# Spill x unscaled and scale it in parts, run the fourth up unit by quarter products, and project dt with v

## What is computed

```python
# layer 0, input projection: dt is the last 16 columns of w_in
u = h @ p["w_in"]
q1, q2, k1, k2, v, z, xbc, dt = jnp.split(u, cuts, axis=-1)
xbc = jax.nn.silu(centred_dwconv(xbc, p["conv_w"], p["conv_b"]))
dt = jax.nn.softplus(dt + p["dt_bias"].reshape(-1))
...
# both layers, after the mixer
x = layer_norm(ALPHA * x + m[2] * d, p["ln1_g"], p["ln1_b"])
f = jnp.square(jax.nn.relu(modulate(x, m[3], m[4]) @ p["w_up"])) @ p["w_down"]
x = layer_norm(ALPHA * x + m[5] * f, p["ln2_g"], p["ln2_b"])
```

## Time and profile before

| what | value |
|---|---|
| median of three runs | 1444.24 us |
| span of the profiled execution | 1442.8 us |
| TensorE busy | 1397.0 us, 97% of the span |
| TensorE weight loads busy | 1240.1 us, 86% |
| VectorE busy | 1040.2 us, 72% |
| ScalarE busy | 543.1 us, 38% |
| GpSimd busy | 77.3 us, 5% |
| mean granted TensorE clock | 0.997 |
| chain that ended last, by engine | PE 79%, DVE 10%, ACT 5% |

### The profile page before, as it was taken

How to read it: one execution, slowest core, us unless ns; L and a number is a source line. 1 busy time by engine, 2 the same in 40 slices (tenths; PEclk the granted TensorE clock), 3 DMA queues, 4 the chain that set the end, 5 groups by cost and what they waited for, 6 DMA issues and landing times.

```text
span 1442.8 us, 22837 instructions
## 1 busy us (share of the span) xinstructions
PE 1397.0 (97%) x8806; PEld 1240.1 (86%) x8806; DVE 1040.2 (72%) x1651; ACT 543.1 (38%) x982; POOL 77.3 (5%) x146
## 2 busy tenths in 40 slices
PE   4999999999999999999999999999999999999996
PEld 3899988766779998998899879888999889989985
DVE  3694566777568876776776796877887677667778
ACT  4333343367454332332232254434443223223322
POOL 1300000010201000000000111001000000000011
PEclk9999999999999999999999999999999999999998
DMA  9701234696713312321221723551332122123141
GB/s 316 232 30 60 88 118 133 213 310 228 265 45 137 126 59 83 94 87 59 87 88 58 268 88 114 185 185 37 146 103 85 62 88 88 59 87 116 59 160 73
DMA packets 132300, 177.47 MB, mean 123 GB/s; under 512 B 4170, under 2 KB 104258, under 8 KB 131698
## 3 DMA queue, kind: packets, MB, share of 16 engines
q1 hardware_dynamic: 123250, 146.46, 31.4%
q0 software_dynamic: 7376, 26.76, 5.3%
q10 hardware_dynamic: 1584, 3.01, 0.6%
HBM read 166.94 MB, written 9.27 MB: 122 GB/s over the span
## 4 chain that ended last, share of the span: by engine, by line
PE 79%; DVE 10%; ACT 5%; issue 2%; DMA 2%; SPq 1%; POOL 0%; ACTq 0%; DVEq 0%
PE ps L801 40%; PE ps L1325 20%; PE ps L783 5%; PE ps L792 4%; PE ps L832 2%; DVE convT L2024 2%; PE ps L1133 2%; DVE wlo L1926 1%; ACT h_full L1722 1%; SPq L570 1%; DVE p_pad L2691 1%; DMA raw_more<-in_w_mod_l 1%; ACT tmp L1722 1%; ACT whi L1430 1%; PE ps L1144 1%
## 5 line engine op out<-in xcount | busy, mean ns | idle before, releaser
L1430 ACT ACTIVATE whi<-raw 128x512 fp32r<-128x512 f32 (+2 forms) x193 | 178.6, 935 | 357.8 <-PE ps L801 293.6
L801 PE MATMUL ps<-whi,hid_hi 128*128 128x512 f32 x640 | 249.6, 390 | 0.0
L801 PE MATMUL ps<-wlo,hid_hi 128*128 128x512 f32 x640 | 249.2, 389 | 0.0
L801 PE MATMUL ps<-whi,hid_lo 128*128 128x512 f32 x640 | 249.1, 389 | 0.0
L1926 DVE TENSOR_TENSOR wlo<-raw,whi 128x512 fp32r<-128x512 f32 (+2 forms) x193 | 204.9, 1070 | 26.0 <-ACT whi L1430 22.5
L2357 DVE TENSOR_TENSOR acc<-acc,ps 128x512 f32<-128x512 f32 x120 | 80.2, 684 | 122.0 <-PE ps L801 122.0
L801 PE MATMUL ps<-whi,h_hi 128*128 128x256 f32 (+1 forms) x480 | 157.4, 328 | 2.5 <-DVE wlo L1926 1.4
L801 PE MATMUL ps<-whi,h_lo 128*128 128x256 f32 (+1 forms) x480 | 152.9, 319 | 0.0
L801 PE MATMUL ps<-wlo,h_hi 128*128 128x256 f32 (+1 forms) x480 | 152.8, 318 | 0.0
L801 PEld LDWEIGHTS ps<-whi,hid_hi 128*128 128x128 f32 x640 | 120.1, 188 | 25.4 <-DVE wlo L1926 0.8
L801 PEld LDWEIGHTS ps<-whi,hid_lo 128*128 128x128 f32 x640 | 120.1, 188 | 25.1
(11 more groups left out here) (339 smaller groups left out, 2654.6 us busy)
## 6 DMA issues: line engine op xcount, KB each, us to landing
raw<-in_w_up_l SPq DMA_DIRECT2D x32, 1024.0 KB, 5.6
raw<-in_w_down_l SPq DMA_DIRECT2D x32, 1024.0 KB, 4.9
raw<-in_w_mod_l SPq DMA_DIRECT2D x26, 1024.0 KB, 5.8
raw<-in_w_in_l SPq DMA_DIRECT2D x12, 1024.0 KB, 5.2
raw_split<-in_w_mod_l SPq DMA_DIRECT2D x8, 1024.0 KB, 6.7
raw<-in_w_out_l SPq DMA_DIRECT2D x6, 1024.0 KB, 5.9
x_spill<-x_tok POOLq DMA_DIRECT2D x10, 512.0 KB, 2.9
x_tok<-x_spill POOLq DMA_DIRECT2D x10, 512.0 KB, 6.2
```

Of the source, the lines that this page charges most:

```text
L801: mm = pe.matmul(out, a_of(still, k), w_of(part, k), start=(first and k == 0 and part == 0 and still == 0), stop=(last and k == nk - 1 and ...
L1430: act.activation(ring_piece(whi, w, g), piece(w, g), ACT.Copy).then_inc(hi_done, 1)
```

## The change

**x in parts.** `rescale` in the MLP is gone. Pool spills each tile as soon as PE has turned it, unscaled. When all five have landed, ten parts of 128 tokens by 512 columns go one after the other through two buffers that lie in the place of the MLP's gate: load, scale on DVE (two operations on 512 columns), store to the same place, wait for the store, load the part after next. g and b are loaded for 512 columns at a time, the second time when part 4 is scaled. On DVE parts 0 to 3 stand behind groups of downs 0 and 1, parts 4 to 9 behind groups of downs 2 and 3. The gate is spread after the tenth part.

**Unit 3 by quarter products.** SU goes from 4 to 3. The token sums stand behind the first units, the weight sums and halves of unit 3 beside unit 2. The ring's halves are assigned anew, as there are three whole units ahead in place of four.

**dt with v.** dt's 16 columns stand behind the 256 of the first v block in buffers of their own, so the first five groups have 272 columns. ACT copies 16 columns more of each of them. The dt stage and `turn_dt` are gone. The split of block 5 on DVE goes ahead of the convolution of block 7, and the tanh of blocks 6 and 7 on ACT behind groups 2 and 4; the ACT steps of softplus stand at groups 4, 5 and 7 in place of 4, 6 and 8. Counts of semaphores follow.

```diff
--- before.py
+++ after.py
...
         tmp = at("tmp", 192, [P, 2, D])
+        part_g, part_b, part_x0, part_x1 = (at(name, 168 + 2 * n, [P, 512]) for n, name in
+                                            enumerate(("part_g", "part_b", "part_x0", "part_x1")))
+        part_x = (part_x0, part_x1)
...
-        wdt2 = at("wdt_halves", 168.5, [P, KT, 32], F32R)
+        wv = [at(name, kb, [P, KT, BW + 16], F32R) for name, kb in (("v_dt_hi", 48), ("v_dt_lo", 108))]
...
-        SU, NS_UP, CONV_UP = 4, 12, 8
+        SU, NS_UP, CONV_UP = 3, 13, 6
...
-        PAR = [w % 2 for w in W_UP]
...
+        def half(w):
+
+            return (w + sum(w > u + SU for u in W_UP)) % 2
+
+        PAR = [half(w + SU) for w in W_UP]
...
-            r = [4 * (w % 2) + n for n in range(4)]
+            r = [4 * half(w) + n for n in range(4)]
...
+            if w == W_V:
+                return (wv[0] if buf is whi else wv[1])[:, :, 0:BW]
             ap = at_ring(buf, ring(w)[g])
...
             def spill_x(layer):
 
                 for t in range(NT):
-                    pool.wait_ge(ln_x, 2 * NT * layer + t + 1)
+                    pool.wait_ge(ln_tr, 2 * NT * layer + t + 1)
                     pool.dma_start(A["x_spill"][t * P:(t + 1) * P, :], x[:, t, :]).then_inc(x_re, 16)
 
+            def part_in_memory(n):
+
+                cols = slice(n // NT * 512, n // NT * 512 + 512)
+                return A["x_spill"][n % NT * P:(n % NT + 1) * P, cols]
...
+            def load_part(layer, n):
+
+                if n % NT == 0:
+                    pool.wait_ge(ln_x, 3 * NT * layer + n)
+                    for which, dst in (("g", part_g), ("b", part_b)):
+                        pool.dma_start(dst[:], A[f"ln1_{which}_l{layer}"][n // NT * 512:n // NT * 512 + 512]
+                                       .partition_broadcast(P)).then_inc(gb_ld, 16)
+                pool.dma_start(part_x[n % 2][:], part_in_memory(n)).then_inc(part_ld[n % 2], 16)
+
+            def scale_parts(layer):
+
+                spilled = 16 * NT * (4 * layer + 2)
+                pool.wait_ge(x_re, spilled)
+                load_part(layer, 0)
+                load_part(layer, 1)
+                for n in range(2 * NT):
+                    pool.wait_ge(ln_x, 3 * NT * layer + n + 1)
+                    pool.dma_start(part_in_memory(n), part_x[n % 2][:]).then_inc(x_re, 16)
+                    pool.wait_ge(x_re, spilled + 16 * (n + 1))
+                    if n + 2 < 2 * NT:
+                        load_part(layer, n + 2)
+
             def fetch_x_again(layer):
 
                 pool.wait_ge(up_mm, UPS * layer + CONV_UP + NS_UP * NPROD)
-                pool.wait_ge(x_re, 16 * NT * (2 * layer + 2))
                 for t in range(NT):
                     pool.dma_start(x[:, t, :], A["x_spill"][t * P:(t + 1) * P, :]).then_inc(x_re, 16)
-                load_gb(2 * layer + 1)
...
             def mlp(layer):
 
                 spill_x(layer)
+                scale_parts(layer)
+                spread_gate(2 * layer + 1)
                 fetch_x_again(layer)
 
-            load_gb(0)
             norm_share(0)
-            spread_gate(1)
             mlp(0)
...
-            pe.wait_ge(dt_wl, 1)
-            pe.wait_ge(mod_row, M_MIX)
-            pe.wait_ge(mod_out, M_MIX)
-            for k in range(KT):
-                for part, n in ((1, 16), (0, 32)) if k else ((0, 32), (1, 16)):
-                    for hf in range(2):
-                        mm = pe.matmul(ps[0:n, (6 + hf) * 512:(6 + hf) * 512 + HALF], wdt2[:, k, 0:n],
-                                       HP[part][:, k, hf * HALF:(hf + 1) * HALF],
-                                       start=(k == 0 and part == 0), stop=(k == KT - 1 and part == 0))
-            mm.then_inc(dt_row, 1)
...
-            def turn_dt():
-
-                pe.wait_ge(dt_cp, 1)
-                rows = dtT[:].rearrange("p a n -> p (a n)")
-                for t in range(NT):
-                    mm = pe.transpose(bank(6, 32 * t, 32 * t + 32), rows[0:32, t * P:(t + 1) * P], ident[0:32, 0:32])
-                mm.then_inc(dt_mm, 1)
...
+                if ib == 0:
+                    pe.wait_ge(dt_wl, 1)
+                    tokens_still(bank(4 + g % 2, 0, BW + 16), h_tile(HP, t), lambda part, k: wv[part][:, k, :], KT) \
+                        .then_inc(ib_mm, 1)
+                    return
...
-                if g == 1:
-                    turn_dt()
...
-                    if u == SU and item == 0:
-                        pe.wait_ge(relu_ok[layer], 8 * (layer + 1))
+                    if u == SU and item in (0, 2):
+                        pe.wait_ge(relu_ok[layer], 2 * SU * (layer + 1) - (1 if item == 0 else 0))
...
-                    if f >= 1:
+                    if 1 <= f < KT - 1:
                         conv_tanh(f - 1)
...
+                if ib == 0:
+                    act.activation(dx[:, 16 * t:16 * t + 16], bank(4 + g % 2, BW, BW + 16), ACT.Copy)
                 act.activation(v[:, 2 + t, ib * BW:(ib + 1) * BW], bank(4 + g % 2, 0, BW), ACT.Copy).then_inc(v_ev, 1)
...
-                if g == 1:
-                    conv_tanh(KT - 1)
+                if g in (2, 4):
+                    conv_tanh(KT - 3 + g // 2)
                 if g == 4:
                     act.wait_ge(dt_v, 2)
...
-                if g == 6:
+                if g == 5:
...
-                if g == 8:
+                if g == 7:
...
+                if g == 8:
...
-                        split_hi(w + 1)
+                        split_hi(w + 1, None, (0, 1, 2))
                         relu_square(layer, 2 * n)
-                        if n == 3:
-                            for m, (k0, hf) in enumerate(((4, 1), (0, 0), (0, 1), (4, 0))):
-                                high_t(layer, m, k0, hf)
+                        for m, (k0, hf) in enumerate(((4, 1), (0, 0), (0, 1), (4, 0))):
+                            high_t(layer, m, k0, hf)
                         relu_square(layer, 2 * n + 1)
+                        split_hi(w + 1, None, (3, 4, 5))
                         continue
...
+                    if f == 5:
+                        dve.wait_ge(dt_w, 2)
+                        dve.tensor_tensor(wv[1][:, :, BW:BW + 16], wdt[:], wv[0][:, :, BW:BW + 16].bitcast(F32),
+                                          ALU.subtract).then_inc(dt_wl, 1)
+                    if f == KT - 1:
+                        split_lo(5)
                     conv(f)
                     if f >= 1:
                         conv_silu(f - 1)
-            split_lo(5)
             conv_silu(KT - 1)
...
+            dve.wait_ge(v_ev, NT)
+            dve.tensor_tensor(dx3, dx3, db[:, 0, :].unsqueeze(1).to_broadcast([P, NT, 16]), ALU.add).then_inc(dt_v, 1)
             dve.wait_ge(dt_v, 1)
-            mark(dve.tensor_tensor(dx3, dx3, db[:, 0, :].unsqueeze(1).to_broadcast([P, NT, 16]), ALU.add))
...
+            def scale_part(layer, n):
+
+                dve.wait_ge(gb_ld, 32 * (3 * layer + n // NT + 1))
+                dve.wait_ge(part_ld[n % 2], 16 * (NT * layer + n // 2 + 1))
+                mark(dve.tensor_tensor(part_x[n % 2][:], part_x[n % 2][:], part_g[:], ALU.mult))
+                settle()
+                dve.tensor_tensor(part_x[n % 2][:], part_x[n % 2][:], part_b[:], ALU.add).then_inc(ln_x, 1)
...
                 dve.wait_ge(t_hi, 4 * layer + n + 1)
-                if n == 0:
-                    dve.wait_ge(ln_x, NT * (2 * layer + 1))
                 if n == 2:
...
-                    if n >= 4:
-                        rescale(2 * layer, n - 4)
+                token_sums(layer)
...
-                        split_lo(w + 1)
+                        weight_sums(w + 1)
+                        split_lo(w + 1, None, (0, 1, 2))
+                        dve.wait_ge(gate_out, 16 * (2 * layer + 2))
                         square_low(layer, 2 * n)
-                        if n == 2:
-                            rescale(2 * layer, 4)
-                        else:
-                            low_t(layer, 0, 4, 1, tlo[:, 0])
-                            low_t(layer, 1, 0, 0, tlo[:, 1])
+                        low_t(layer, 0, 4, 1, tlo[:, 0])
+                        low_t(layer, 1, 0, 0, tlo[:, 1])
                         square_low(layer, 2 * n + 1)
-                        if n == 2:
-                            token_sums(layer)
-                        else:
-                            low_t(layer, 2, 0, 1, hhi[:, 0:4, HALF:TOK])
-                            low_t(layer, 3, 4, 0, hlo[:, 0:4, HALF:TOK])
-                            dve.wait_ge(t_lo, 4 * (layer + 1))
+                        low_t(layer, 2, 0, 1, hhi[:, 0:4, HALF:TOK])
+                        split_lo(w + 1, None, (3, 4, 5))
+                        low_t(layer, 3, 4, 0, hlo[:, 0:4, HALF:TOK])
+                        dve.wait_ge(t_lo, 4 * (layer + 1))
...
                     for t in range(NT):
                         down_group(layer, n, t, i)
```

(4 more changed lines are left out.)

58 lines of the change are left out of this document (21 added, 37 removed).

## The result

The kernel after the change takes **1456.85 us** (median; 1455.98 to 1459.12), the kernel before 1444.68 beside it: a ratio of 1.0087, with a 95% interval of 1.0073 to 1.01. The prediction was 1441.8 with a range up to 1447.0, so it is 15.0 us off; 0.4 of them are that the kernel before took 1444.68 beside it and not 1444.24. The profiled execution has a span of 1454.8 us, 12.0 more than before. First the page's part 1, which answers to the earlier trace rows; TensorE has 61 matmuls less, and is busy for 2.2 us more.

A forecast was written before the change was run, and what follows sets the result against it. TensorE, with work in 97% of the span, was taken to bound the kernel. The terms -4.7 + 2 x (0.85 + 0.3) = -2.4 us gave a 1441.8 us median, range 1436.5 to 1447.0.

The forecast's parts named there:

- Part 1: v block: dt's columns join the first five groups, group 2 starts at 102.0 instead of 107.11; gain 4.7 us.
- Rival C: v blocks: ScalarE 2 us later than walked, group 7 waits, dt gain falls to about 2.7; 1443.8 us, chance 0.09.
- Part 2: MLP unit 3 by seven quarter products: +0.85 us a layer in place of -1.76, bounds -1.76 and +2.5.
- the walk: ScalarE's and VectorE's queues followed on paper with old durations; units 2 and 3 end at 492.35 against 491.48.
- TensorE's clock I leave alone: MLP: clock taken as staying 2.4 GHz, since a stretch with 1.8 of 8 us idle was granted 1.00.
- Rival A: Unit 3: ScalarE and VectorE finish beside unit 2 in time, each layer gains 1.76 us; 1436.0 us, chance 0.18.
- Part 3: Ten parts of x scaled behind the down blocks: +0.3 us a layer, bounds 0 and 8.
- the round trip of a part: Downs 2 and 3: storing and reloading a 256 KB part, taken as 2.7 + 2.8 = 5.5 us.
- rival B: Downs 2 and 3: VectorE waits for parts 5 and 9, unit 6 late; chance 0.19 nearer case, 0.06 far.
- The slack: Before unit 6's sixth product: VectorE's first combination could come 2.6 us later free; delay expected 2.2 to 2.9.
- B's nearer case: Downs 2 and 3: part loads take 3.8 us, costing some 2.2 us a layer; 1445.6 us, chance 0.19.
- B's far end: Downs 2 and 3: part loads take 6.2 us, six parts lose 5 to 8 us a layer; 1451 to 1457, chance 0.06.

The follow-up runs named there:

- e1: Kernel before with only dt's columns moved into the first v block, MLP and x as before: 1439.86 us, 0.9967; 1440.66 us, 0.9971 when run again.
- e4: Changed kernel with 12 and 11 unread matmuls filling TensorE's idles before unit 3's fourth product and down 3's last group: 1454.23 us, 1.0062.
- e5: Changed kernel with 6 and 6 unread matmuls in the idles, in place of e4's 12 and 11: 1451.57 us, 1.0042.
- e6: Changed kernel without the parts' stores and reloads, VectorE's operations on them kept, so the result differs: 1445.76 us, 1.0002.
- e3: Changed kernel with part 4 scaled behind down 1's last group and parts 5 to 9 spread over downs 2 and 3: 1447.47 us, 1.0016.
- e2: Changed kernel with ScalarE's relu and square of block 5 ahead of the third and fourth high halves of the tokens: 1450.46 us, 1.0031.
- e7: Changed kernel with the reorderings of e2 and e3, plus VectorE's third low half ahead of block 5's square and low half: 1442.66 us, 0.9974.
- e8: e7 with VectorE's fourth low half of the tokens moved behind the first two combinations of unit 3: 1441.38 us, 0.9979.
- e9: e8 with 32 more already met waits a layer on Pool, behind the ten parts: 1441.23 us, 0.9982.
- e12: e1 with 20 more transfers a layer on Pool's queue behind the spill of x, each waiting for the one before: 1518.4 us.

## Why the prediction was wrong, step by step

**Part 1 was right.** Group 2 was to start at 102.0, released by ScalarE's copy, after 0.8 us of idle; it starts at 102.59 after 0.62, and at 101.45 in e1. The gain was to be 4.7 us; it is 4.6 in the profile and 0.33% in e1 (0.33% of 1445 is 4.8). That the profile comes so close is in part luck: behind the v block it is 4.1, and the start of group 2 alone varies by 1.1 us between profiles. The other 0.5 arise near 365 us, where the chain of the kernel before has a wait for a weight load. Rival C is out: no idle in groups 5 to 9.

**Part 2: the walk was right, the clock was not.** The walk gave an idle of 2.2 us ahead of the fourth product (measured 1.87), one of 0.25 ahead of the sixth (0.2 in e4), and down 0 at 29.03, which is 0.87 more than before. Where the clock stays, in e4, e5 and layer 0 of e6, a is 29.10 to 29.12. The step that failed is the sentence "TensorE's clock I leave alone", which rested on the earlier trace rows. I took it for proof that an idle of this size is harmless. It was no proof: the 1.78 us of idle in that stretch are one piece, from 430.12 to 431.90, and the stretch ends with it, so it shows the clock ahead of the idle and not behind it. In this one profile the clock held behind it too, but in the same place of e3, in the same work, it fell (first the kernel before, then e3: the timeline row with the idle, and a window behind it):

```profile
431.90 0.38 PE L792 MATMUL ps<-h_hi,whi 128*128 128x320 f32 x1 [1.78 <-DVE h_lo L2416]
432.00:434.00 2.00, 2.00 (x14) 1.00 1.02 354
...
426.42 0.38 PE L827 MATMUL ps<-h_hi,whi 128*128 128x320 f32 x1 [1.81 <-DVE h_lo L2431]
428.00:430.00 2.00, 2.00 (x9) 0.50 0.37 129
```

Over the fourteen profiles the clock fell behind 6 of the 28 idles of that kind (1.77 to 1.87 us, one a layer), and behind 5 of the 6 of 1.87 us ahead of unit 3's fourth product. Why it is one in five there and nearly every time here stays open. The fall cost 1.3 us a layer net of what it hid, and a is 30.44. Rival A could not happen either: e2, e7 and e8 take the order's fault away in three ways, and a doesn't fall below 27.76, because VectorE's work there is more than TensorE's. I had named ScalarE as what speaks against A; it was VectorE.

**Part 3: the mis-sized term is the round trip of a part whose transfers meet others.** The mechanism is rival B's: VectorE waits for parts 5, 6 and 9. VectorE's timeline after, in downs 2 and 3:

```profile
555.14 0.69 DVE L2436 TENSOR_TENSOR part_x<-part_x,part_g 128x512 f32<-128x512 f32 x1 [5.18 <-DMA part_x<-x_spill]
...
559.03 0.69 DVE L2436 TENSOR_TENSOR part_x<-part_x,part_g 128x512 f32<-128x512 f32 x1 [1.28 <-DMA part_x<-x_spill]
...
573.54 0.69 DVE L2436 TENSOR_TENSOR part_x<-part_x,part_g 128x512 f32<-128x512 f32 x1 [2.59 <-DMA part_x<-x_spill]
...
579.82 1.00 DVE L2517 TENSOR_TENSOR tmp<-tmp,ps 128x320 f32<-128x320 f32 x2
```

To compare with the walk, 2.29 us have to be added, as this stretch lies that much earlier. Part 4 ended at 550.8 (as walked). Part 5's data came at 557.4 (555.7), part 6 was done at 562.7 (559.7), part 7 at 569.5 (566.5), part 9's data at 575.8 (572.1), and VectorE was free at 577.2 (573.5). So of the 3.7 us, 3.0 arose with parts 5 and 6, where I had walked three loads and nothing for the store behind them. Pool's timeline shows why:

```profile
550.10 0.54 POOL L757 DMA_DIRECT2D part_x<-x_spill  x1
550.63 0.54 POOL L767 DMA_DIRECT2D x_spill<-part_x  x1
555.99 0.54 POOL L757 DMA_DIRECT2D part_x<-x_spill  x1 [4.81 <-DMA x_spill<-part_x]
```

Part 4's store is issued behind the loads of g, b and part 5, beside the last 0.3 MB of a weight load of 1 MB; it lands after 5.08 us, against the 2.7 of the earlier trace rows that I took for every store, and only then may part 6 be loaded. Whether the loads ahead of it or the weight load beside it slow it more, the runs don't separate: in e3, which has no g and b there, part 5's store beside the weight load alone still takes 5.14 us in layer 0 and 4.21 in layer 1. The store of part 7, beside no such load, took 2.30, and its whole round trip 6.0 (I had 5.5). The Trainium skill, DMA: Bandwidth & Descriptors, section Queues, rings and completion order, says that each DMA engine takes turns between the queues it has work for, packet by packet. The traces agree in so far as a store of a part lands later with other transfers beside it. From issue to landing such stores took 2.3 us with nothing beside them; 2.4 to 5.1 with one other transfer of Pool; 3.2 to 3.6 in sixteen that met 0.7 MB of a weight load, and 4.2 to 5.1 in eight that met 0.9 MB; and behind three loads of Pool 5.0 to 6.4 beside the end of a weight load, as here, and 6.4 to 8.9 beside a whole one (part 4's store in e3 and e7 to e9).

The slack was 2.6 us, so 5.9 us of delay (3.7 over the walk's 2.2) had to show as an idle of about 3; it shows as 2.58 in unit 6 and 0.41 in down 3. Up to there the loss is 3.0 us a layer, past B's nearer case (2.2). The clock fell behind this idle too, 15.84 us of matmuls in 17.64, 1.8 us more a layer. So b lost 5.1 and 5.0 us, and the time lies in the band of B's far end (5 to 8 us a layer, 1451 to 1457), to which I had given 0.06. It is there by another way: that case had loads of 6.2 us and nothing of the clock; the loads of parts 6 and 9 took 2.95 and 3.33.

**The end.** Nothing in my sum stood for the 2.05 us behind the last work, by which Pool's DRAIN is longer (9.99 us for 7.95). I costed Pool's 22 added transfers a layer by what they hide behind, not by what they do to the end of the program.

**The sum again, by its terms:** dt -4.6 for -4.7; unit 3 2 x 2.3 for 2 x 0.85; the parts 5.1 + 5.0 for 2 x 0.3; the end +2.05 for 0. That is +12.1 for -2.4, and the spans differ by 12.0. Of the 14.4 us of the span that were missed, 6.3 are the clock (1.33 and 1.8 a layer), about 6 the later transfers, and 2 the end.

**What to make of the change.** Part 1 alone has the lowest times here, 0.9967 and 0.9971 of before in two sets of runs. The rest of the change, mended in three and four orders, is at 0.9974 (e7) and 0.9979 (e8). The intervals overlap, so this is no gain over part 1 alone, and no clear loss: unit 3 by quarter products brings 0.4 us a layer of its 1.76, b is 0.25 longer, and the transfers take 2 at the end.

## What to carry to other kernels

An idle on a busy TensorE has two prices: its length, and what the granted clock does behind it; a pause of 2 us cost 1.3 to 1.8 us more where the clock fell behind it, so price each such idle twice. A clock that held in one stretch of one profile proves little: look at what comes behind the idle, and at the same idle in other profiles, as the clock fell behind it in some and not in others. When work moves off TensorE, add up the whole load of the engine that gets it over the same stretch before walking its order; where the load is over TensorE's time, no order helps. For a small transfer in a chain of waits, look up which large one runs beside it, and put the hand-over where an engine has other work for the whole round trip (e3 won 9 us by moving one part ahead and spreading the others). And look at the end of the program: an engine's transfers can have a price there that no stage shows.

## What the runs showed of the hardware

- **The clock falls behind some idles and not behind others of the same length.** TensorE, busy at 2.4 GHz before, was granted 1.2 GHz for 3.4 us after all four idles of 2.29 to 2.63 us (unit 6 of the kernel after and of e2) and after 11 of 35 of 1.77 to 1.94 us (the fourth product of unit 3, 5 of 6; the norm ahead of the MLP, 6 of 28; layer 1 of e4, 0 of 1); in the two of 34 and 37 us of e12 it fell during the idle. After none of the shorter ones, of 0.25 to 1.44 us, did it fall (all fourteen profiles, from 60 us on). The fall began between 0.5 us before work had begun again and 1.5 us after. The Trainium skill, TensorE: Matmul & The Clock Gate, section What's actually happening, says that the chip watches TensorE on a schedule of its own, so that the point of a change varies from run to run. The two layers of e6 agree with that.
- **A slow clock hides another engine's lateness.** With the clock kept at 1.00 in e4, 1.77 us of slow matmuls gave back only 1.33, as VectorE was next.
- **Small stores beside other transfers.** 256 KB stored from Pool's queue, from issue to landing: 2.3 us alone; 3.2 to 5.1 beside a weight load of 1 MB; 5.08, 5.34 and 6.44 beside one and behind three loads of Pool's own queue.
- **The end of the span grows with the transfers on Pool's queue.** Pool's closing DRAIN takes 7.95 us, and 0.3 us more with 4 transfers added, 1.7 with 40 and 2.0 with 44. They stood behind the spill in e12 and beside the down blocks in the kernel after. 200 more waits on Pool's queue did not change it.
